# Hand-overs between normed stages: row sums kept with tokens on partitions, the factor spread by scaled identities, own rooms for two weight units

## The chip, the core and the metric

One core of a Trainium2 chip runs the whole program. The metric is device time in microseconds (us) of one execution. Before the change, three timed executions took 3216.22, 3218.62 and 3218.68 us; the median is 3218.62.

## The reference

Two transformer blocks of depth 2 run one after the other on one sequence of T = 512 tokens, model width D = 1024, in float32. The first (`ffn1`, `mix`, `ffn2`, twice) is not touched. The second has four stages, each of the form

```
h = h + rms_norm(f(rms_norm(h, gain_pre)), gain_post)
rms_norm(x, g) = x * rsqrt(mean(x * x over the 1024 channels) + 1e-6) * g
f: diff  differential attention (w_qkv, w_o)
   conv_0  h @ w_in (1024 x 5632), causal conv of width 3, gelu(gate) * val, @ w_out (2816 x 1024)
   fox   forgetting attention with shared keys, values and gates (w_kvf, w_q, w_o)
   conv_1  as conv_0
```

So between two stages two norms follow each other: the *post* norm of what the stage gave, added to the residual stream, and the *pre* norm of the sum, which feeds the next stage's products. The output is the stream after `conv_1`.

## The kernel before

Activations lie with channels on partitions: `xres`, `acc`, `h_hi` and `h_lo` are [128, 8, 512], eight channel blocks (k) of 512 tokens. Each product is made in three passes, high weight by high input, high by low, low by high, so ScalarE (`hi`, L817) copies a raw weight unit into its high part and VectorE (`lo`, L1293) subtracts to get the low part. A unit `c` is one 128-column block of a weight matrix; units are numbered through the program, and a unit's raw room, high and low rooms and PSUM bank are those of `c % 2`. SyncE issues the load of unit c when `lo` of unit c-2 is done (`load`, L539). `hi(c)` waits until TensorE is done with unit c-2, whose rooms it takes. Every engine works through one program order written out by hand; semaphores join them.

A pre norm is applied late: TensorE multiplies the un-normed `h_hi`/`h_lo` = gain times x, and the factor `rstd` (one per token, the same on all partitions) multiplies the result when VectorE takes it out of PSUM (`divided`, L1399). A post norm needs its factor `rstd2` at once.

The three hand-overs (`diff` to `conv_0`, `conv_0` to `fox`, `fox` to `conv_1`; `CHAINED` and `HALVED` name the stages before and after) and the end after `conv_1` run in two halves of 256 tokens:

- TensorE, `finish` (L1986): the last two output units, first for tokens 0 to 255, then for 256 to 511 (L2011). In the second part, at block nk//2, it issues `half_stat` for the first half, and behind its end `half_stat` for the second. `half_stat` (L1977, L1983) sums squares over channels: a full matrix of ones (weights) times [128 x 256] squares, so all 128 partitions hold the sum of each token. GpSimd has summed the squares of the first six blocks in `ssq`; ScalarE squares the last two (`half_square`, L869).
- ScalarE, `half_root` (L879): square root on [128 x 256]. VectorE, `half_invert` (L1358, L1362): reciprocal on [128 x 256].
- Then, block by block: VectorE makes `norm_t` = acc * gain * rstd2 (`post`, L1383), GpSimd adds it to `xres` (L800), ScalarE makes `h_hi` (L858) and the squares of the new x (L860), VectorE makes `h_lo` (`half_low`, L1334), three blocks behind `norm_t`.
- TensorE, `gemm_halves` (L1942): units c and c+1 of the next stage block by block as `h_lo` comes, with the pre norm's statistics between them, the second unit two blocks behind the first. Then unit c+2 in full width (`gemm`, L1905).

VectorE's order in `post` (L1365) holds `half_take` (the last two output units' halves out of PSUM, L1348 or L1350), the reciprocals and the low parts of units c and c+1; ScalarE's order in `finish` (L882) holds the matching squares, roots and high parts. After `conv_1`, TensorE transposes x (L2430), ScalarE copies it out of PSUM (L1268) and SyncE stores it.

## Time and profile before

| | |
|---|---|
| median of three timed executions | 3218.62 us |
| span of the profiled execution | 3216.7 us |
| TensorE busy (matmuls) | 3158.3 us, 98% of the span |
| VectorE / ScalarE / GpSimd busy | 54% / 36% / 17% |
| hand-over diff to conv_0 (2149.7 to 2190.7) | 41.0 us, granted clock 0.92 |
| hand-over conv_0 to fox (2527.1 to 2570.7) | 43.6 us, granted clock 0.96 |
| hand-over fox to conv_1 (2802.9 to 2843.8) | 40.9 us, granted clock 0.92 |
| end (3180.3 to 3216.7) | 36.4 us, granted clock 0.82 |

The profiled execution's own time outside the profiler is not given apart from the three; its span is 1.9 us under their median and 0.5 above the shortest. A hand-over is read here from the first half-width matmul of the old stage's last two units to the first full-width matmul of unit c+2 of the new stage. Times of a row are its start and its duration; matmuls overlap in the pipeline, so their spacing is read from start to start.

### The profile page before, as it was taken

What the parts mean: (1) busy time and instruction counts of PE and PEld (TensorE: products, weight loads), DVE (VectorE), ACT (ScalarE), POOL (GpSimd) and SP (SyncE); (2) the same over time, 40 slices, a digit from 0 to 9 for tenths busy, and PEclk for the clock granted to TensorE, in tenths of its full rate; (3) what the DMA queues carried; (4) which work ended last, traced back from release to release, by engine and by line L of the source; (5) the groups of instructions that cost most, each with busy time, mean ns of one, the idle gap of its engine ahead of it and who ended that gap; (6) DMA issues with size and microseconds to landing.
All of it is one profiled execution on the core that took longest, in us unless ns stands there. A gap on an engine that the chain in (4) does not pass through costs nothing.

```text
span 3216.7 us, 42242 instructions
## 1 busy us (share of the span) xinstructions
PE 3158.3 (98%) x14778; PEld 2537.6 (79%) x14778; DVE 1744.4 (54%) x2707; ACT 1160.1 (36%) x1880; POOL 534.5 (17%) x482
## 2 busy tenths in 40 slices
PE   8999999999999999999999999999999999999998
PEld 6888876788888888776888878668888886778887
DVE  4434477543445434585543453557656546586474
ACT  4323246322223222354322232644324335443242
POOL 0000336200020000265100030231000422310004
PEclk9999999999999999999999999999999999999999
DMA  4355331333333333321333323112333231223332
GB/s 122 97 143 148 95 108 36 89 97 93 98 98 93 104 91 106 80 60 47 94 104 90 108 76 118 47 55 77 107 88 102 66 103 40 60 72 104 92 96 81
DMA packets 528363, 288.01 MB, mean 90 GB/s; under 512 B 13603, under 2 KB 520198, under 8 KB 528256
## 3 DMA queue, kind: packets, MB, share of 16 engines
q1 hardware_dynamic: 523648, 273.32, 29.4%
q0 software_dynamic: 4608, 13.30, 1.4%
q8 instruction: 62, 1.02, 0.1%
q14 instruction: 45, 0.37, 0.0%
HBM read 284.30 MB, written 10.02 MB: 91 GB/s over the span
## 4 chain that ended last, share of the span: by engine, by line
PE 86%; DVE 7%; issue 3%; ACT 3%; POOL 1%; DMA 0%; DVEq 0%; ACTq 0%; POOLq 0%
PE bank L1905 66%; PE bank L1918 5%; PE bank L2075 3%; PE bank L2185 2%; PE bank L1935 2%; PE bank L2227 2%; PE bank L2250 1%; PE bank L2011 1%; PE bank L1964 1%; DVE w_lo L1293 1%; ACT w_hi L817 1%; PE bank L1983 1%; DVE scaled_g L1399 0%; DVE tap_g L1488 0%; DVE norm_t L1383 0%
## 5 line engine op out<-in xcount | busy, mean ns | idle before, releaser
L817 ACT ACTIVATE w_hi<-w_raw 128x1024 fp32r<-128x1024 f32 (+2 forms) x477 | 534.0, 1119 | 1419.3 <-PE bank L1905 718.8
L1905 PE MATMUL bank<-h_hi,w_hi 128*128 128x512 f32 x2420 | 949.2, 392 | 7.4 <-DVE h_lo L1323 3.7
L1905 PE MATMUL bank<-h_hi,w_lo 128*128 128x512 f32 x2420 | 942.4, 389 | 0.0
L1905 PE MATMUL bank<-h_lo,w_hi 128*128 128x512 f32 x2408 | 937.7, 389 | 0.0
L1293 DVE TENSOR_TENSOR w_lo<-w_raw,w_hi 128x1024 fp32r<-128x1024 f32 (+1 forms) x445 | 616.0, 1385 | 526.1 <-ACT w_hi L817 526.1
L1905 PEld LDWEIGHTS bank<-h_hi,w_hi 128*128 128x128 f32 x2420 | 453.7, 187 | 115.1 <-issue 14.7
L1905 PEld LDWEIGHTS bank<-h_hi,w_lo 128*128 128x128 f32 x2420 | 453.8, 188 | 95.9
L1905 PEld LDWEIGHTS bank<-h_lo,w_hi 128*128 128x128 f32 x2408 | 451.7, 188 | 95.5 <-issue 1.9
L1905 PE MATMUL bank<-act_hi,w_hi 128*128 128x512 f32 x924 | 360.3, 390 | 0.0
L1905 PE MATMUL bank<-act_lo,w_hi 128*128 128x512 f32 x924 | 360.0, 390 | 0.0
L1905 PE MATMUL bank<-act_hi,w_lo 128*128 128x512 f32 x924 | 359.9, 390 | 0.0
L1905 PEld LDWEIGHTS bank<-act_hi,w_hi 128*128 128x128 f32 x924 | 173.8, 188 | 36.3 <-issue 0.2
L1905 PEld LDWEIGHTS bank<-act_lo,w_hi 128*128 128x128 f32 x924 | 173.9, 188 | 36.2
L1905 PEld LDWEIGHTS bank<-act_hi,w_lo 128*128 128x128 f32 x924 | 173.8, 188 | 36.2
L1419 DVE SCALAR_TENSOR_TENSOR xres<-bank,xres 128x512 f32 (+1 forms) x64 | 44.2, 691 | 248.0 <-PE bank L1905 248.0
L1399 DVE TENSOR_TENSOR scaled_g<-bank,rstd 128x512 f32<-128x512 f32 x132 | 91.2, 691 | 149.6 <-PE bank L1905 144.8
L660 POOL TENSOR_TENSOR ssq<-xres 128x512 f32<-128x512 f32 x6 | 6.2, 1041 | 969.8 <-DVE xres L1419 945.8
L938 ACT ACTIVATE gated<-scaled_g 128x512 f32<-128x512 f32 x88 | 55.6, 632 | 297.3 <-DVE scaled_g L1399 297.2
L663 POOL TENSOR_TENSOR ssq<-ssq,psq 128x512 f32<-128x512 f32 x62 | 135.9, 2191 | 4.9
L1464 DVE TENSOR_TENSOR prod<-gate_r,bank 128x512 f32<-128x512 f32 x88 | 60.5, 687 | 99.2 <-PE bank L1905 99.0
L660 POOL TENSOR_TENSOR ssq<-acc 128x512 f32<-128x512 f32 x4 | 4.2, 1040 | 636.4 <-DVE acc L1426 619.2
L718 POOL TENSOR_TENSOR w_lo<-w_raw,w_hi 128x1024 fp32r<-128x1024 f32 x32 | 76.8, 2399 | 184.7 <-ACT w_hi L817 184.7
(333 smaller groups left out, 4160.8 us busy)
## 6 DMA issues: line engine op xcount, KB each, us to landing
w_raw<-in_ffn_w_gate_dram SPq DMA_DIRECT2D x88, 512.0 KB, 3.8
w_raw<-in_ffn_w_up_dram SPq DMA_DIRECT2D x88, 512.0 KB, 3.8
w_raw<-in_ffn_w_down_dram SPq DMA_DIRECT2D x64, 704.0 KB, 4.6
w_raw<-in_ffn_w_in_dram SPq DMA_DIRECT2D x88, 512.0 KB, 3.8
w_raw<-in_ffn_w_out_dram SPq DMA_DIRECT2D x32, 704.0 KB, 4.7
w_raw<-in_w_in_dram SPq DMA_DIRECT2D x34, 512.0 KB, 3.8
w_raw<-in_a_w_qkv_dram SPq DMA_DIRECT2D x24, 512.0 KB, 3.8
w_raw<-in_w_out_dram SPq DMA_DIRECT2D x16, 512.0 KB, 3.8
```

The source lines that it names most:

```text
L663: add = nc.gpsimd.tensor_tensor(ssq[:, :], ssq[:, :], psq[:, :], ALU.add)
L718: nc.gpsimd.tensor_tensor(w_lo[c % 2][:, 0:KT, :], raw[c % 2][:, 0:KT, :], w_hi[c % 2][:, 0:KT, :].bitcast(f32), ALU.subtract).then_inc(lo ...
L817: nc.scalar.activation(split_home(c)[0][:, 0:nk, 0:cols], raw[c % 2][:, 0:nk, 0:cols], ACT.Copy).then_inc(hi_ready, 1)
L1293: nc.vector.tensor_tensor(w_low[:, 0:nk, 0:cols], raw[c % 2][:, 0:nk, 0:cols], w_high[:, 0:nk, 0:cols].bitcast(f32), ALU.subtract).then_in ...
L1399: nc.vector.tensor_tensor(dst, result(c)[rows, :], rstd[rows, :], ALU.mult).then_inc(bank_free[c % 2], 1)
L1464: nc.vector.tensor_tensor(prod[:, :], gate_r[:, :], result(at + 1)[:, :], ALU.mult).then_inc(bank_free[(c + 1) % 2], 1)
L1905: mm = nc.tensor.matmul(result(c)[0:cols, :], w[:, k, 0:cols], x[k], start=(k == 0 and n == 0), stop=(k == nk - 1 and n == 2))
L1918: mm = nc.tensor.matmul(bank[c % 2][:, :], w[c % 2][:, k, :], x[k], start=(k == 0 and n == 0), stop=(k == KT - 1 and n == 2))
L1935: mm = nc.tensor.matmul(result(u)[:, :], w[u % 2][:, k, :], x[k], start=(k == 0 and n == 0), stop=(k == nk - 1 and n == 2))
L2075: mm = nc.tensor.matmul(V_BANK[t][:, :], x[:, k, tok], of_block[w][j], start=(k == 0 and n == 0), stop=(k == KT - 1 and n == 2))
L2185: mm = nc.tensor.matmul(PAIR_S[x][:, at:at + w], job["q"][:, P * i:P * (i + 1)], job["k"][:, first:first + w], start=True, stop=alone)
L2227: mm = nc.tensor.transpose(TURN[s % 2][:, to:to + P], ring_of(stage)[(2 * p + x) % 4][:, col:col + P], ident[:, :])
```

## The change

At the four places, not elsewhere:

- The statistic is turned. The squares are now the weights (128 channels x 128 tokens) and one column of `mean_p` (every value 1/128) is the moving operand, so the sum of each token lands on that token's partition, one PSUM column for 128 tokens. A block of a half takes two such matmuls instead of one with 256 columns.
- The root works on [128 x 2], the reciprocal too (`norm_tok`). VectorE then makes two scaled identities, diag(factor), in `rms`, and TensorE multiplies a matrix of ones with them (`half_spread`), which puts the factor on all partitions again, in PSUM. The post norm's `norm_t` reads the factor from PSUM there (`SPREAD_POST`); for the pre norm ScalarE copies it to `rstd` (`spread_copy`).
- Units c and c+1 of the next stage get rooms of their own (`home`), laid over the bias tables, so their `hi` waits for no matmul. `hi` and `lo` of both units move ahead of the first half's root and reciprocal; those of unit c+2 move into `finish` and to the end of `post`. On GpSimd `fox`'s writes into that area wait for the first two units.
- In the hand-overs the post norm's second statistic and its spread move from the end of `finish` into `gemm_halves`, to blocks 3 and 6 of the first half; the pre norm's spreads stand behind block 7 of the second half and at block 3 of unit c+2. `half_take` of the second half moves to blocks 1 and 4 of the first. The output transposes use banks 3, 4, 0, 1 instead of 3 to 6.

```diff
@@ -227,6 +232,9 @@
 bias_diff = put("bias_diff", [P, 8, T], bias_at + 4 * HA * NEAR)
+home = [[put(f"home_{part}{i}", [P, KT, P], bias_at + 4 * D * (2 * n + i), f32r) for i in range(2)]
+        for n, part in enumerate(("hi", "lo"))]
+HOMES = {BASE[n] + i for n in HALVED for i in range(2)}
@@ -340,8 +349,11 @@
 HALF = [slice(0, T // 2), slice(T // 2, T)]
-STAT_HALF = [STATB[:, HALF[0]], OUT[:, HALF[1]]]
+STAT_TOK = [STATB[:, T // 2:T // 2 + 2], OUT[:, 0:2]]
+SPREAD_POST = [bank[5][:, HALF[0]], bank[6][:, HALF[1]]]
+SPREAD_NEXT = [STATB[:, HALF[0]], OUT[:, HALF[1]]]
 EARLY_HALF = [bank[3], bank[4]]
+Y_BANK = [bank[3], bank[4], bank[0], bank[1]]
@@ -404,6 +417,8 @@
+if c in HOMES:
+    return home[0][c % 2], home[1][c % 2]
@@ -761,6 +776,7 @@
 pool.wait_ge(o_ready, OUTB["fox"])
+pool.wait_ge(mm_done, BASE["fox"] + 2)
@@ -811,8 +827,8 @@
     act.wait_ge(*also)
-if c >= 2 and c not in THIRD:
-    act.wait_ge(mm_done, c - 1 + 2 * j)
+if c >= 2 and c not in THIRD and c not in HOMES:
+    act.wait_ge(mm_done, c - (3 if c - 2 in HOMES else 1) + 2 * j)
@@ -869,38 +885,49 @@
-def half_root(event, n, half):
+def half_root(event, half):
...
         act.wait_ge(sum_ready, STAT[event] + 1)
-    nc.scalar.activation(rms[:, HALF[half]], STAT_HALF[half], ACT.Sqrt, bias=eps_c[:, 0:1],
-                         scale=1.0 / n).then_inc(rms_ready if half else rms_first, 1)
+    nc.scalar.activation(norm_tok[:, int(event in BASE), 2 * half:2 * half + 2], STAT_TOK[half], ACT.Sqrt,
+                         bias=eps_c[:, 0:1], scale=P / D).then_inc(rms_ready if half else rms_first, 1)
+def spread_copy(name, half):
+    act.wait_ge(spread_done, SPREAD_DONE[name, half])
+    nc.scalar.activation(rstd[:, HALF[half]], SPREAD_NEXT[half],
+                         ACT.Copy).then_inc(rstd_ready if half else rstd_first, 1)
 def finish(name):
...
     half_square(name, 0, 0)
+    hi(c)
+    hi(c + 1)
     half_square(name, 0, 1)
-    half_root("post_" + name, D, 0)
-    hi(c)
+    half_root("post_" + name, 0)
     half_square(name, 1, 0)
-    hi(c + 1)
-    half_square(name, 1, 1)
     following = NEXT.get(name)
     if following is None:
-        half_root("post_" + name, D, 1)
+        half_square(name, 1, 1)
+        half_root("post_" + name, 1)
         return
...
             if half == 0 and k == 2:
-                half_root("post_" + name, D, 1)
+                half_square(name, 1, 1)
+            if half == 0 and k == 4:
+                half_root("post_" + name, 1)
+            if half == 1 and k == 2:
+                half_root(following, 0)
             if half == 1 and k == 4:
-                half_root(following, D, 0)
+                hi(c + 2)
+    spread_copy(following, 0)
 def act_high(jj):
@@ -1170,13 +1197,15 @@
     token_root()
-hi(c + 2)
+if name not in HALVED:
+    hi(c + 2)
...
 elif name in HALVED:
+    half_root(name, 1)
     hi(c + 3)
-    half_root(name, D, 1)
+    spread_copy(name, 1)
@@ -1265,7 +1294,7 @@
 act.wait_ge(y_turned, 2 * t + a + 1)
-nc.scalar.activation(ytok[:, t, T * a:T * (a + 1)], bank[3 + 2 * (t % 2) + a][:, :],
+nc.scalar.activation(ytok[:, t, T * a:T * (a + 1)], Y_BANK[2 * (t % 2) + a][:, :],
@@ -1350,17 +1379,17 @@
-def half_invert(event, half):
-    dst = (rstd if event in BASE else rstd2)[:, HALF[half]]
+def half_diag(event, half):
+    tok = norm_tok[:, int(event in BASE), :]
...
         dve.wait_ge(rms_first, HALF_ROOT[event] + 1)
-        nc.vector.reciprocal(dst, rms[:, HALF[0]]).then_inc(rstd_first, 1)
-        dve.wait_ge(rstd_first, HALF_ROOT[event] + 1)
...
         dve.wait_ge(rms_ready, ROOT[event] + 1)
-        nc.vector.reciprocal(dst, rms[:, HALF[1]]).then_inc(rstd_ready, 1)
-        dve.wait_ge(rstd_ready, ROOT[event] + 1)
+    chain(nc.vector.reciprocal(tok[:, 2 * half:2 * half + 2], tok[:, 2 * half:2 * half + 2]))
+    for t in (2 * half, 2 * half + 1):
+        ins = nc.vector.tensor_scalar(rms[:, P * t:P * (t + 1)], ident[:, :], tok[:, t:t + 1], None, ALU.mult)
+    ins.then_inc(diag_ready if half else diag_first, 1)
 def post(name, how):
@@ -1368,30 +1397,37 @@
     half_take(name, how, 0, 0)
+    lo(c)
     half_take(name, how, 0, 1)
-    half_invert("post_" + name, 0)
-    half_take(name, how, 1, 0)
-    lo(c)
+    lo(c + 1)
+    half_diag("post_" + name, 0)
+    dve.wait_ge(rstd_first, HALF_ROOT["post_" + name] + 1)
     lag = 3
...
         for k in range(KT + lag):
+            if half and k == 0:
+                if name not in NEXT:
+                    half_diag("post_" + name, 1)
+                dve.wait_ge(rstd_ready, ROOT["post_" + name] + 1)
             if k < KT:
...
                     dve.wait_ge(x_done, X_FIRST[name] + k - 3)
-                nc.vector.scalar_tensor_tensor(norm_t[k % 4][:, tok], acc[:, k, tok], gain(g, l, k), rstd2[:, tok],
+                nc.vector.scalar_tensor_tensor(norm_t[k % 4][:, tok], acc[:, k, tok], gain(g, l, k), SPREAD_POST[half],
                                                ALU.mult, ALU.mult).then_inc(t_ready if half else t_first, 1)
-            if half == 0 and k == 2:
+            if half == 0 and k == 1:
+                half_take(name, how, 1, 0)
+            if half == 0 and k == 4:
                 half_take(name, how, 1, 1)
...
                 half_low(NEXT[name], k - lag, half)
-            if half == 0 and k == 4:
-                lo(c + 1)
-            if half == 0 and k == 6:
-                half_invert("post_" + name, 1)
+            if half == 0 and k == 8 and name in NEXT:
+                half_diag("post_" + name, 1)
+            if half == 1 and k == 7 and name in NEXT:
+                half_diag(NEXT[name], 0)
     if name in NEXT:
-        half_invert(NEXT[name], 0)
+        lo(c + 2)
 def divided(c, dst, j=0, rows=slice(0, P)):
@@ -1780,13 +1816,15 @@
     continue
-lo(c + 2)
+if name not in HALVED:
+    lo(c + 2)
...
 elif name in HALVED:
+    half_diag(name, 1)
     lo(c + 3)
-    half_invert(name, 1)
+    dve.wait_ge(rstd_ready, ROOT[name] + 1)
@@ -1891,7 +1929,7 @@
 def _(pe):
-    def gemm(c, x_hi, x_lo, ready, count, j=0):
+    def gemm(c, x_hi, x_lo, ready, count, j=0, midway=None):
@@ -1900,6 +1938,8 @@
 for k in range(nk):
+    if midway is not None and k == 3:
+        half_spread(midway, 1)
@@ -1945,6 +1985,12 @@
 for k in range(KT + lag):
+    if half == 0 and k == 3:
+        half_stat("post_" + before, 1, [b[:, HALF[1]] for b in sq_last])
+    if half == 0 and k == 6:
+        half_spread("post_" + before, 1)
+    if half == 1 and k == KT:
+        half_spread(name, 0)
     if k < KT:
@@ -1960,30 +2006,45 @@
 def half_block(c, k, tok, last):
     cols = UNIT[c][1]
-    for n, (w, x) in enumerate(((w_hi, h_hi), (w_hi, h_lo), (w_lo, h_hi))):
-        mm = nc.tensor.matmul(result(c)[0:cols, tok], w[c % 2][:, k, 0:cols], x[:, k, tok],
+    w_high, w_low = split_home(c)
+    for n, (w, x) in enumerate(((w_high, h_hi), (w_high, h_lo), (w_low, h_hi))):
+        mm = nc.tensor.matmul(result(c)[0:cols, tok], w[:, k, 0:cols], x[:, k, tok],
                               start=(k == 0 and n == 0), stop=(k == KT - 1 and n == 2))
...
 def half_stat(event, half, blocks, at=0, n=None):
-    if half == 0 and at == 0:
+    summed = event in POOL_SUM
+    if half == 0 and summed:
         stat_free(event)
-    summed = event in POOL_SUM
     if summed:
...
             pe.wait_ge(ssq_ready, POOL_SUM[event] + 1)
-        nc.tensor.matmul(STAT_HALF[half], ones[:, :], ssq[:, HALF[half]], start=True, stop=False)
+        for j in range(2):
+            nc.tensor.matmul(STAT_TOK[half][:, j:j + 1], ssq[:, P * (2 * half + j):P * (2 * half + j + 1)],
+                             mean_p[:, 0:1], start=(j == 0), stop=False)
     for k, b in enumerate(blocks, at):
...
             pe.wait_ge(sq_ready, SQ_FIRST[event] + k + 1)
-        mm = nc.tensor.matmul(STAT_HALF[half], ones[:, :], b, start=(k == 0 and not summed),
-                              stop=(k == (n or len(blocks)) - 1))
+        for j in range(2):
+            mm = nc.tensor.matmul(STAT_TOK[half][:, j:j + 1], b[:, P * j:P * (j + 1)], mean_p[:, 0:1],
+                                  start=(k == 0 and j == 0 and not summed),
+                                  stop=(j == 1 and k == (n or len(blocks)) - 1))
     if k == (n or len(blocks)) - 1:
...
+def half_spread(event, half):
+    pe.wait_ge(diag_ready if half else diag_first, (DIAG[event] if half else HALF_ROOT[event]) + 1)
+    mm = nc.tensor.matmul((SPREAD_NEXT if event in BASE else SPREAD_POST)[half], ones[:, :], rms[:, HALF[half]],
+                          start=True, stop=True)
+    if event in BASE:
+        mm.then_inc(spread_done, 1)
+    else:
+        mm.then_inc(rstd_ready if half else rstd_first, 1)
 def finish(name, x_hi, x_lo, ready, count):
@@ -2005,13 +2066,17 @@
                 pe.wait_ge(ready, count + k + 1)
-                if (half, s, k) == (1, 0, nk // 2):
+                if (half, s, k) == (1, 0, 3):
                     half_stat("post_" + name, 0, [b[:, HALF[0]] for b in sq_last])
+                if half and s * nk + k == 8:
+                    half_spread("post_" + name, 0)
...
             mm.then_inc(mm_done if half else half_done, 1)
-    half_stat("post_" + name, 1, [b[:, HALF[1]] for b in sq_last])
+    if name not in NEXT:
+        half_stat("post_" + name, 1, [b[:, HALF[1]] for b in sq_last])
+        half_spread("post_" + name, 1)
 def first_units(name, c, count):
@@ -2324,7 +2389,7 @@
 first_units(name, c, h0)
-gemm(c + 2, H_HI, H_LO, h_ready, h0)
+gemm(c + 2, H_HI, H_LO, h_ready, h0, midway=name if name in HALVED else None)
...
```

## Rows read from the trace of the kernel before

**Rows 1.** The page: the chain that ended last, share of the span by engine.

```profile
PE 86%; DVE 7%; issue 3%; ACT 3%; POOL 1%; DMA 0%; DVEq 0%; ACTq 0%; POOLq 0%
```

**Rows 2.** Windows: first and second hand-over; busy us (instructions) by engine, clock, DMA.

```profile
2149.70:2190.70 41.00, 36.52 (x238) 33.52 (x236) 32.00 (x44) 19.79 (x45) 17.50 (x18) 0.92 0.16 48
2527.10:2570.70 43.60, 40.12 (x273) 36.73 (x272) 32.32 (x44) 21.15 (x46) 22.62 (x24) 0.96 0.14 37
```

**Rows 3.** Windows: inside the first hand-over.

```profile
2164.00:2168.00 4.00, 1.79 (x9) 1.13 (x8) 3.65 (x7) 3.42 (x10) 3.64 (x5) 1.00 0.46 131
2168.00:2176.00 8.00, 6.15 (x24) 5.46 (x23) 7.96 (x13) 3.63 (x10) 2.84 (x5) 0.57 0.22 66
```

**Rows 4.** Waits of PE in the first hand-over: total, times, longest.

```profile
PE bank L1964 <- DVE h_lo L1334: 2.8, 3, 1.9
PE bank L1983 <- ACT sq_last L869: 1.3, 1, 1.3
PE bank L2011 <- DVE w_lo L1293: 0.3, 1, 0.3
```

**Rows 5.** Timeline of PE: start, duration, engine, line; a statistic, six products follow, then the next.

```profile
2184.63 0.59 PE L1983 MATMUL bank<-acc,ones 128*128 128x256 f32 x2
...
2185.65 0.28 PE L1964 MATMUL bank<-h_hi,w_lo 128*128 128x256 f32 x1
2185.77 0.38 PE L1983 MATMUL bank<-acc,ones 128*128 128x256 f32 x1
```

**Rows 6.** Timeline of PE in diff: eight one-column passes, and what follows.

```profile
2030.02 0.95 PE L2117 MATMUL bank<-mean_p,proj 128*128 128x1 f32 x8
2030.90 0.59 PE L2185 MATMUL bank<-proj 64*128 64x384 f32 x2
```

**Rows 7.** Timeline of DVE in the first hand-over.

```profile
2159.51 1.75 DVE L1358 RECIPROCAL rstd<-rms 128x256 f32<-128x256 f32 x1 [2.88 <-ACT rms L879]
...
2162.77 1.75 DVE L1383 SCALAR_TENSOR_TENSOR norm_t<-acc,gains,rstd 128x256 f32<-128x256 f32 x3
...
2167.44 1.75 DVE L1293 TENSOR_TENSOR w_lo<-w_raw,w_hi 128x1024 fp32r<-128x1024 f32 x1
```

**Rows 8.** Timeline at the program's start: DVE's small reciprocal, scaled identities; ACT's small root.

```profile
28.18 0.18 DVE L1755 RECIPROCAL tok_sum<-tok_sum 128x4 f32<-128x4 f32 x1 [4.58 <-ACT tok_sum L1143]
28.39 0.88 DVE L1757 TENSOR_SCALAR rms<-ident,tok_sum 128x128 f32<-128x128 f32 x4
...
27.86 0.28 ACT L1143 ACTIVATE tok_sum<-tok_sum,eps_c 128x4 f32<-128x4 f32 x1
```

**Rows 9.** Timeline of ACT and DVE in the first hand-over: the two parts of the input.

```profile
2165.91 0.49 ACT L858 ACTIVATE h_hi<-xres,gains 128x256 fp32r<-128x256 f32 x1
...
2167.05 0.47 DVE L1334 SCALAR_TENSOR_TENSOR h_lo<-xres,gains,h_hi 128x256 fp32r<-128x256 f32 x1
```

**Rows 10.** Timeline of SP: load of unit c+1's raw weights; the page: loads' time to landing.

```profile
2153.13 0.37 SPq L539 DMA_DIRECT2D w_raw<-in_ffn_w_in_dram  x1
...
w_raw<-in_ffn_w_in_dram SPq DMA_DIRECT2D x88, 512.0 KB, 3.8
```

**Rows 11.** Timeline of DVE and POOL: norm_t, then a PSUM-reading add, each beside POOL.

```profile
2181.38 0.96 DVE L1383 SCALAR_TENSOR_TENSOR norm_t<-acc,gains,rstd 128x256 f32<-128x256 f32 x1
2181.14 0.91 POOL L800 TENSOR_TENSOR xres<-xres,norm_t 128x256 f32<-128x256 f32 x1 [0.36 <-DVE norm_t L1383]
...
2544.46 0.42 DVE L1350 TENSOR_TENSOR acc<-bank,acc 128x256 f32<-128x256 f32 x1 [0.21 <-PE bank L2011]
2543.05 2.46 POOL L800 TENSOR_TENSOR xres<-xres,norm_t 128x256 f32<-128x256 f32 x3 [11.08 <-DVE norm_t L1383]
2545.88 0.73 POOL L800 TENSOR_TENSOR xres<-xres,norm_t 128x256 f32<-128x256 f32 x1 [0.36 <-DVE norm_t L1383]
```

**Rows 12.** Timeline of DVE and POOL at the end.

```profile
3202.23 6.94 DVE L1383 SCALAR_TENSOR_TENSOR norm_t<-acc,gains,rstd 128x256 f32<-128x256 f32 x9
...
3202.79 7.64 POOL L800 TENSOR_TENSOR xres<-xres,norm_t 128x256 f32<-128x256 f32 x9 [0.99 <-DVE norm_t L1383]
```

More of the change, by code:

```diff
@@ L137, in program @@
     HALF_ROOT, HALF_SQ, half_squares = {}, {}, 0
+    DIAG = {}
     STAT, ROOT, POOL_SUM, SQ_FIRST, X_FIRST, NEXT = {}, {}, {}, {}, {}, {}
@@ L149, in program @@
             HALF_ROOT[n], HALF_SQ[n] = len(HALF_ROOT), half_squares
+            DIAG[n] = HALF_ROOT[n]
             half_squares += KT
@@ L167, in program @@
             HALF_ROOT["post_" + n], HALF_SQ["post_" + n] = len(HALF_ROOT), half_squares
+            DIAG["post_" + n] = HALF_ROOT["post_" + n]
             half_squares += 2
             X_FIRST[n] = KT * len(X_FIRST)
+    SPREAD_DONE = {(n, half): 2 * i + half + 1 for i, n in enumerate(HALVED) for half in range(2)}
     T_FIRST = {n: KT * i for i, n in enumerate(n for n in stages if n in CHAINED)}
@@ L297, in program @@
         own_rows = put("own_rows", [P, 2, NP])
+        norm_tok = put("norm_tok", [P, 2, NT])
         ident, ones = put("ident", [P, P]), put("ones", [P, P])
@@ L366, in program @@
         sum_ready, rms_ready, rstd_ready = sem("sum_ready"), sem("rms_ready"), sem("rstd_ready")
+        diag_first, diag_ready, spread_done = sem("diag_first"), sem("diag_ready"), sem("spread_done")
         t_ready, hhi_ready, h_ready = sem("t_ready"), sem("hhi_ready"), sem("h_ready")
@@ L2404, in _ @@
                     first_units(name, c, h0)
-                    gemm(c + 2, H_HI, H_LO, h_ready, h0)
+                    gemm(c + 2, H_HI, H_LO, h_ready, h0, midway=name)
                     gemm(c + 3, H_HI, H_LO, h_ready, h0)
@@ L2429, in _ @@
                             wait_x(pe, stages[-1], k)
-                        mm = nc.tensor.transpose(bank[3 + 2 * (t % 2) + a][:, P * (k % 4):P * (k % 4 + 1)],
+                        mm = nc.tensor.transpose(Y_BANK[2 * (t % 2) + a][:, P * (k % 4):P * (k % 4 + 1)],
                                                  xres[:, k, P * t:P * (t + 1)], ident[:, :])
```

## The prediction

> **What bounds the kernel now.** Read first the chain that ended last: 86% of the span is TensorE [rows 1], so a microsecond of TensorE work, added or removed, counts in full, and what can be won are TensorE's gaps. The windows give the first two hand-overs 41.0 and 43.6 us [rows 2]; the third, 40.9 at a clock of 0.92, is like the first and stands in the table of times. To see how much of that is gap I work out TensorE's full-speed work there. From one statistic's start to the next, with six half-width products between, is 1.14 us; the last product starts 0.12 before the next statistic, so six products take 0.72 and a statistic (two passes) 0.42 to 0.43 [rows 5]. The first hand-over has 2 x 2 x 8 x 3 = 96 half-width products in the old stage's last two units, 96 in the new stage's first two, and 3 + 3 + 16 = 22 statistics: 192 x 0.12 + 22 x 0.43 = 32.5. The second has 11 blocks in the old units, so 228 x 0.12 + 9.5 = 36.8. The third equals the first. Gap: 8.5, 6.8 and 8.4, together 23.7 us.
>
> Where it lies shows in two views. The waits name 4.4 us in the first hand-over: 2.8 for `h_lo`, 1.3 for the square of the last block, 0.3 for a low weight part [rows 4]. The other 4 us stand in no wait. After 2164 TensorE was busy 1.8 of 4 us, and in the next 8 us its granted clock was 0.57 [rows 3], that is mostly the lower of its two levels, 1.2 of 2.4 GHz: products cost double there. Over whole hand-overs the granted clock was 0.92, 0.96 and 0.92 [rows 2], 3.3 + 1.7 + 3.3 = 8.3 us, part of the 23.7. VectorE was busy 7.96 of those 8 us [rows 3]: it was the late one.
>
> **The change, step by step** (first hand-over; the profiled span, 3216.7, is 1.9 below the median, and I take the difference found there off the median).
>
> *Root and reciprocal small.* A reciprocal on 128x256 took 1.75 [rows 7], on 128x4 0.18; a scaled identity 0.88/4 = 0.22; the small root 0.28 [rows 8]. Root, reciprocal and two identities come to 0.28 + 0.18 + 0.44 = 0.9, plus hand-overs between engines, against 1.75 for the reciprocal and a root at half width before it. Then TensorE spreads in two passes like a statistic, 0.43.
>
> *TensorE's added work.* Statistics: eight one-column passes take 2030.02 to 2030.90 = 0.88 [rows 6]; a block of a half needs four, 0.44 against 0.43. So the turned statistic saves TensorE nothing; 66 of them cost up to 1.0 more in all. Spreads: 4 per hand-over, 12 x 0.43 = 5.2. Sum 6.2 us on the path.
>
> *Earlier factor.* `hi` of unit c+1 now stands ahead of the second half-square in ScalarE's queue. Its load is issued at 2153.13 and lands 3.8 later, 2156.9 [rows 10]; a high part and the square, some 1.5 together, end at 2158.4. TensorE reaches that square at 2153.0 + 24 x 0.12 + 9 x 0.12 + 0.88 = 2157.9: a new stall of 0.5. In the second hand-over the old units are 36 products longer, the load is in, and nothing waits. The statistic ends at 2158.85, root and identities at 2160.0, the spread is issued at block 8, 2160.65, and the first `norm_t` can start at 2161.3 instead of 2162.8 [rows 7]. The low parts of c and c+1 (1.75 for the one that stood in the middle of the chain at 2167.44 [rows 7]) now end before the factor is there: VectorE waited then, so they cost nothing.
>
> *The feed of `gemm_halves`.* The old units end at 2164.0 (one spread later than before). `norm_t` 2161.3 plus 0.47, GpSimd 0.73 [rows 11], `h_hi` 0.49 and `h_lo` 0.47 [rows 9], with what ScalarE has queued, gives 2164.2: 0.2 stall. But VectorE's `half_take` of the last unit stands at block 4, ahead of the second `h_lo`, and cannot start before that unit's products are out, 2164.6. Then 0.42 + 0.47 for `h_lo` 1 and 0.94 for `norm_t` 5 and `h_lo` 2: TensorE waits 1.0 and 0.6. From block 2 on it has 1.15 of work per block against 0.95 to 1.28 for VectorE. In the second half `hi(c+2)`, about 1.1 in ScalarE's row, holds back block 5; with the diagonal's 0.6 in VectorE's I count 0.6 (0.3 to 1.2). The second spread waits for TensorE's own block 6; from there to the second half's first `h_lo` takes 2.9, TensorE still has 2 x 1.15 + 2 x 0.8 = 3.9: covered, by 1.0.
>
> Left over: 0.3 + 0.5 + 0.2 + 1.6 + 0.6 = 3.2 in the first and third, 0.95 + 0.6 + 0.6 = 2.15 in the second, where the factor is early. Together 8.5. With idle never over 1.0 at a time and TensorE busy over half of every 2 us, I take it that the clock stays up.
>
> *After it.* `lo(c+2)` ends before c+2 is due. Spread and copy of the pre norm's second half lie in unit c+2, 0.43 of which I counted; the factor is out some 3.2 us after that unit's start, before it was 3.9. GpSimd's new wait in `fox` holds back only writes of tables that are read long after.
>
> *`norm_t` from PSUM.* With both tensors in SBUF it took 0.96 beside GpSimd's add, which itself took 0.91; a VectorE add with one operand in PSUM took 0.42 beside a busy GpSimd, and GpSimd's shorter adds are 0.73 [rows 11]. So the bounds for `norm_t` are 0.42 and 0.96; I take 0.47. The Trainium skill (SBUF — State Buffer, "Who interferes with whom") says that a VectorE instruction with two SBUF inputs contends with a GpSimd one that reads SBUF and one with at most one doesn't. The rows agree. By its rule in full the pace in the second halves would be GpSimd's alone; that is the case "no gap left" below.
>
> *End.* The same steps for `conv_1`: the factor of the first half comes about 1.2 sooner, which the wait for the last unit swallows. The second half can start when the last unit is out (0.43 later than before), squared and summed: 3199.5, root and diagonals 3200.9, spread 3201.35, `norm_t` 3201.5. Before, nine `norm_t` in 6.94 from 3202.23 [rows 12] put the second half's first at 3203.0. From there GpSimd paces: nine in 7.64 is 0.85 each [rows 12]. Gain 1.5 plus 0.2 of 0 to 1.0 for a faster GpSimd: 1.7. The two spreads are inside this.
>
> **Sum.** 23.7 - 8.5 - 6.2 + 1.7 = 10.7 us less: 3218.6 - 10.7 = 3208.
>
> **Rivals.**
> 1. *No gap left.* `half_take` is not late because `norm_t` runs at 0.42 and GpSimd at 0.73, and ScalarE's extra high part hides. Left over only 0.3 twice: 23.7 - 0.6 - 6.2 + 2.7 = 19.6, 3199. For: the low add of rows 11. Against: the wait for the last unit's products is no matter of pace.
> 2. *The clock still falls.* The waits shrink to my 8.5 but the clock drops for the same stretches, 8.3 more: 3216, no change that can be measured. For: it fell after 2.2 us of idle in 4 [rows 3], and my stalls are 1.8 within 2.6 us. Against: TensorE works again at full rate right behind them. The Trainium skill (TensorE: Matmul & The Clock Gate, "What's actually happening") says that the throttled state is the default and that activity releases it; by that rule the full clock is not safe while waits remain, which is this rival's time, and no row tells at which of the two my shorter waits end.
> 3. *Slower: the feed is no faster, the work is.* Place: the loop ScalarE, VectorE, TensorE, VectorE that each factor now runs, with TensorE in order. If it and the late `half_take` give back what the small reciprocals save, the gaps stay at 23.7 and 6.2 come on top, with 0.9 at the end: 3226. It is slower from the point where gaps shrink by less than 6.2 of 23.7. Against: VectorE alone loses 5 us of reciprocals and 1.75 of a low part per hand-over from the busy stretch.
>
> **Chances.** Forecast 0.60 (its own range 3203 to 3212, nearly all faster), rival 1 0.14, rival 2 0.17, rival 3 0.09. A change under 0.2%, 6.4 us, can't be told from none: faster means below 3212.2. Faster 0.57 + 0.14 = 0.71 and 0.01 of rival 2: 0.72; same 0.03 + 0.16 = 0.19; slower 0.09. Range 3199 to 3216: it leaves out rival 3, half of rival 1 and a little of rival 2.
>
> **What would show it.** Right: hand-overs of about 38, 41.6 and 38 us; granted clock near 1.0 in them; root and reciprocal rows of 0.2 to 0.3; `norm_t` near 0.47 beside GpSimd; waits for `h_lo` under 2 us per hand-over, right behind the `half_take` at block 4; statistics of 0.44. Wrong: a clock of 0.5 after the first `h_lo`; long waits of `norm_t` in the second half for the spread; a wait over 1 us at the first statistic because a load lands late; statistics well above 0.44.

## The result, and the profile after

| | before | after |
|---|---|---|
| median of eight executions each | 3217.62 us | 3226.39 us |
| range | 3216.22 to 3218.68 | 3223.74 to 3228.63 |
| ratio after/before | | 1.0028, 95% interval 1.0019 to 1.0037 |
| span of the profiled execution | 3216.7 | 3223.5 |

The kernel became slower by 8.8 us, clear of the noise by its interval, where 3208 was forecast with a range of 3199 to 3216.

The windows of the three hand-overs after the change, in the columns of [rows 2]: from the first half-width product of the old stage's last two units to the first full-width product of unit c+2.

```profile
2147.30:2189.30 42.00, 39.91 (x288) 38.76 (x287) 24.69 (x50) 18.59 (x47) 15.97 (x18) 0.88 0.21 59
2526.00:2578.10 52.10, 51.35 (x324) 50.49 (x323) 23.87 (x51) 20.27 (x48) 16.38 (x18) 0.74 0.16 41
2810.60:2852.70 42.10, 39.98 (x288) 38.81 (x287) 24.77 (x50) 20.00 (x48) 16.12 (x18) 0.88 0.20 59
```

Before they took 41.0, 43.6 and 40.9 us [rows 2, and the table of times]; now 42.0, 52.1 and 42.1. Read the first number behind the length (TensorE busy) against the number behind the five busy times (granted clock): TensorE idles for 2.1, 0.75 and 2.1 us where [rows 2] show 4.5 and 3.5 in the first two, and VectorE's work fell from 32 to under 25 us. The gaps that the change was to close are half of what they were or less. But the clock is 0.88, 0.74 and 0.88 instead of 0.92, 0.96 and 0.92. At 0.5 for the lower level (1.2 of 2.4 GHz) that is 42.0 x 0.12 + 52.1 x 0.26 + 42.1 x 0.12 = 23.6 us lost, against 8.3 before.

The waits of TensorE in the first hand-over, to be held against [rows 4]:

```profile
PE bank L2011 <- DVE h_lo L1363: 1.3, 3, 0.9
PE bank L2033 <- ACT sq_last L885: 0.4, 1, 0.4
PE bank L2074 <- DVE w_lo L1322: 0.3, 1, 0.3
```

2.0 us instead of 4.4. Inside the first hand-over (the same place as [rows 3]), and then the second, cut at the places where the clock changes:

```profile
2162.00:2164.00 2.00, 0.94 (x6) 0.77 (x6) 2.00 (x6) 2.00 (x7) 1.31 (x2) 1.00 0.00 0
2164.00:2168.00 4.00, 3.84 (x30) 3.63 (x28) 2.18 (x6) 1.38 (x5) 2.64 (x3) 0.85 0.00 0
2168.00:2176.00 8.00, 8.00 (x38) 7.82 (x37) 3.08 (x10) 1.62 (x5) 0.72 (x2) 0.50 0.00 0
...
2526.00:2549.00 23.00, 22.25 (x184) 21.77 (x183) 13.22 (x25) 11.03 (x24) 9.97 (x10) 1.00 0.26 69
2549.00:2576.00 27.00, 27.00 (x126) 26.73 (x125) 10.64 (x26) 8.54 (x23) 6.41 (x8) 0.50 0.08 20
2576.00:2578.10 2.10, 2.10 (x17) 1.99 (x16) 0.02 (x1) 0.70 (x3) 0.00 (x0) 0.90 0.00 0
```

In the kernel before, the clock stood at half for some 6.6 us of the first hand-over (41.0 x 0.08 x 2) and came back. Now the second hand-over spends 27 us at half clock with TensorE busy in every one of them. VectorE, busy 7.96 of 8 us in [rows 3], is busy 3.1 of 8 here: at half clock TensorE itself is the late one. The sign that the prediction gave for being wrong, a clock of 0.5 after the first `h_lo`, is there.

A statistic and its six products, at full clock and at half, from TensorE's timeline (start, duration); from one statistic's start to the next it is 1.16 us at full clock, against 1.14 in [rows 5], and 2.13 at half clock:

```profile
2180.66 0.50 PE L2033 MATMUL bank<-mean_p,acc 128*128 128x1 f32 x4
...
2181.82 0.50 PE L2033 MATMUL bank<-mean_p,acc 128*128 128x1 f32 x4
...
2170.00 0.85 PE L2033 MATMUL bank<-mean_p,acc 128*128 128x1 f32 x4
...
2172.13 0.85 PE L2033 MATMUL bank<-mean_p,acc 128*128 128x1 f32 x4
```

VectorE in the first hand-over (to be held against [rows 7, 8, 11]): small reciprocal, two scaled identities, `norm_t` from PSUM, `half_take` at block 4 with the `h_lo` behind it, and the second half's first `norm_t`.

```profile
2157.06 0.17 DVE L1389 RECIPROCAL norm_tok<-norm_tok 128x2 f32<-128x2 f32 x1
2157.26 0.48 DVE L1391 TENSOR_SCALAR rms<-ident,norm_tok 128x128 f32<-128x128 f32 x2
2159.05 0.87 DVE L1417 SCALAR_TENSOR_TENSOR norm_t<-acc,gains,bank 128x256 f32<-128x256 f32 x2 [1.30 <-PE bank L2042]
...
2162.35 0.41 DVE L1377 TENSOR_SCALAR acc<-bank 128x256 f32<-128x256 f32 x1
2162.69 0.91 DVE L1363 SCALAR_TENSOR_TENSOR h_lo<-xres,gains,h_hi 128x256 fp32r<-128x256 f32 x1
...
2174.72 1.65 DVE L1417 SCALAR_TENSOR_TENSOR norm_t<-acc,gains,bank 128x256 f32<-128x256 f32 x4 [4.88 <-PE bank L2042]
```

The last row shows what the low clock does to the order: the spread stands in TensorE's own queue, so `norm_t` waits 4.88 us for it.

The end, from the first half-width product to the last instruction, took 3223.5 - 3189.45 = 34.05 us instead of 36.4: 2.35 less. e1 below, with 34.1 us there, has the same gain, so it does not hang on the clock in the hand-overs. Between the hand-overs each stage took 0.2 to 0.3 us more, probably part of the spread that lies in unit c+2. Up to the first hand-over this profiled execution was 2.4 us shorter than that of before, at a clock of 1.00 against 0.98 in its first 200 us; that is not of the change: e2 below, which is the kernel before up to that point, reached it 2.0 us sooner too (2147.7 against 2149.7). Together: +10.7 (hand-overs) + 0.9 - 2.35 - 2.4 = +6.8, the difference of the spans.

### The profile page after: what moved, and what is told of

It is laid out like the page before. It is cut to its first block, busy times and chain, and to the rows that moved or that the text cites. A ratio compares the mean times of both kernels' runs of the same rounds, so it can differ in the third digit from the quotient of the medians.

```text
span 3223.5 us, 42603 instructions
## 1 busy us (share of the span) xinstructions
PE 3174.0 (98%) x14950; PEld 2561.5 (79%) x14950; DVE 1712.4 (53%) x2735; ACT 1156.6 (36%) x1886; POOL 529.6 (16%) x482
## 4 chain that ended last, share of the span: by engine, by line
PE 87%; DVE 6%; issue 3%; ACT 3%; POOL 1%; DMA 0%; DVEq 0%; ACTq 0%; POOLq 0%; SPq 0%
PE bank L1945 66%; PE bank L1958 5%; PE bank L2140 3%; PE bank L2250 2%; PE bank L1975 2%; PE bank L2292 2%; PE bank L2011 2%; PE bank L2315 1%; PE bank L2074 1%; PE bank L2033 1%; ACT w_hi L833 1%; DVE w_lo L1322 1%; ACT tap_v L987 0%; DVE prod L1555 0%; DVE scaled_g L1435 0%
## 5 line engine op out<-in xcount | busy, mean ns | idle before, releaser
L833 ACT ACTIVATE w_hi<-w_raw 128x1024 fp32r<-128x1024 f32 (+1 forms) x471 | 527.6, 1120 | 1396.8 <-PE bank L1945 716.8
L1322 DVE TENSOR_TENSOR w_lo<-w_raw,w_hi 128x1024 fp32r<-128x1024 f32 (+1 forms) x439 | 607.2, 1384 | 517.8 <-ACT w_hi L833 517.7
```

The lines of the kernel that those rows point to most:

```text
L833: nc.scalar.activation(split_home(c)[0][:, 0:nk, 0:cols], raw[c % 2][:, 0:nk, 0:cols], ACT.Copy).then_inc(hi_ready, 1)
L1322: nc.vector.tensor_tensor(w_low[:, 0:nk, 0:cols], raw[c % 2][:, 0:nk, 0:cols], w_high[:, 0:nk, 0:cols].bitcast(f32), ALU.subtract).then_in ...
```

## Experiments

The waits shrank and the clock didn't stay up. Two things could hold it down: the new form of the statistics (one moving column per 128 x 128 weights, where 256 columns moved before), or the stalls at the first blocks, whatever the statistic's form.

**e1, wide operand.** All 128 equal columns of `mean_p` move, not one, into 128 PSUM columns; the root reads one column of each block.

```diff
-STAT_TOK = [STATB[:, T // 2:T // 2 + 2], OUT[:, 0:2]]
+STAT_WIDE = [STATB[:, HALF[1]], OUT[:, HALF[0]]]
+STAT_TOK = [STATB[:, T // 2:T:P], OUT[:, 0:T // 2:P]]
...
-mm = nc.tensor.matmul(STAT_TOK[half][:, j:j + 1], b[:, P * j:P * (j + 1)], mean_p[:, 0:1],
+mm = nc.tensor.matmul(STAT_WIDE[half][:, P * j:P * (j + 1)], b[:, P * j:P * (j + 1)], mean_p[:, :],
```

> The kernel after with one edit: the moving operand of each turned statistic is all 128 equal columns of mean_p instead of one, into 128 PSUM columns per token block instead of 1; the root reads one column of each block as before. In theory A (the one-column passes hold the granted clock at its lower level after the stalls of a hand-over) the stretches at half clock of the three hand-overs, some 10, 27 and 10 us in the kernel after, shrink to 5 us or less each, the windows of the three hand-overs fall from 42.0, 52.1 and 42.1 us to 38 to 40 each, and the time to 3200 to 3212 us (from 3226.4). In theory B (the stalls alone set how long it lasts, whatever the statistic's form) the stretches and the time stay: 3223 to 3229 us. A statistic should still take about 0.44 us per half block at full clock; were it longer by 0.2 the sum would be 13 us worse.

Measured: 3203.9 us, ratio 0.9960 (0.9946 to 0.9974). Its three hand-overs, the stretch with the stalls and the 12 us behind it in the first, the waits of TensorE there, and a statistic with six products:

```profile
2147.00:2184.20 37.20, 35.28 (x288) 34.13 (x287) 24.81 (x50) 18.51 (x47) 16.15 (x18) 1.00 0.23 67
2520.80:2560.30 39.50, 38.76 (x323) 38.14 (x322) 24.39 (x50) 20.15 (x47) 16.58 (x18) 1.00 0.20 54
2792.90:2830.10 37.20, 35.31 (x288) 34.17 (x287) 24.79 (x50) 19.95 (x48) 16.13 (x18) 1.00 0.23 67
...
2161.60:2163.60 2.00, 0.90 (x5) 0.73 (x6) 2.00 (x6) 2.00 (x7) 1.35 (x2) 1.00 0.00 0
2163.60:2167.60 4.00, 3.83 (x34) 3.63 (x32) 2.20 (x7) 1.38 (x5) 2.65 (x3) 1.00 0.00 0
2167.60:2175.60 8.00, 8.00 (x70) 7.95 (x69) 6.44 (x17) 4.94 (x15) 4.26 (x6) 1.00 0.01 2
...
PE bank L2012 <- DVE h_lo L1364: 1.4, 3, 0.9
PE bank L2075 <- DVE w_lo L1323: 0.3, 1, 0.3
PE bank L2034 <- ACT sq_last L886: 0.3, 1, 0.3
...
2170.93 0.61 PE L2034 MATMUL bank<-mean_p,acc 128*128 128x128 f32 x4
...
2172.09 0.61 PE L2034 MATMUL bank<-mean_p,acc 128*128 128x128 f32 x4
```

The same instructions but for the width, the same waits to 0.1 us, the same 1.16 us from statistic to statistic, and the clock is 1.00 in all three. The hand-overs are 4.8, 12.6 and 4.9 us shorter than after the change, 22.3 of the 22.5 us between the medians. The one-column operand cost no time of its own, and with it the clock fell. Stalls of this size (TensorE busy 0.90 of 2 us here, 0.94 after the change) don't make it fall by themselves. Larger ones may: see e9.

**e2, the kernel before with one-column passes.** In its statistics all but the first pass of a sum are two one-column matmuls instead of one with 256. The sums that come of it are wrong, so this kernel computes other factors, and its values differ from there on; it is for timing only.

```diff
-mm = nc.tensor.matmul(STAT_HALF[half], ones[:, :], b, ...)
+for j in range(2):
+    mm = nc.tensor.matmul(STAT_HALF[half][:, j:j + 1], b[:, P * j:P * (j + 1)], ones[:, 0:1], start=False, ...)
```

> The kernel before with one edit: in the statistics of the hand-overs all passes of 256 columns but the first of each sum are replaced by two one-column passes, so that the factors are not the reference's; order, roots, reciprocals and waits stay. Theory A: the low-clock stretches of the hand-overs (6.6, 4 and 6 us before) become 10 us or longer, and the time rises by 5 to 20 us to 3222 to 3238. Theory B: at full clock both forms take 0.43 to 0.44 us, so the time stays at 3217 to 3219 us and the clock of the hand-overs at 0.92, 0.96 and 0.92.

Measured: 3223.99 us (3222.05 to 3236.51), ratio 1.0026 (1.0017 to 1.0035).

```profile
2147.70:2195.00 47.30, 42.81 (x273) 41.38 (x271) 31.72 (x44) 19.48 (x45) 17.44 (x18) 0.78 0.14 41
2531.40:2575.10 43.70, 40.39 (x310) 39.10 (x309) 32.33 (x44) 21.13 (x46) 22.62 (x24) 0.92 0.14 37
2807.30:2848.20 40.90, 36.39 (x274) 35.04 (x272) 31.98 (x44) 21.18 (x46) 17.49 (x18) 0.92 0.17 48
```

The first hand-over, 41.0 before, takes 47.3 with some 20 us at half clock; the second spends some 7 us there (43.7 x 0.08 x 2), twice as long as before, and the third the same as before. It goes the way of the first theory in the other kernel too, but not in every hand-over: what the one-column passes do there depends on something that these rows don't show. Nor does it separate the operand's width from the other values.

**e3, statistics and factors as before, the rest as after.** Ones times 256 columns, root and reciprocal on 128x256, no spreads; rooms and order stay.

```diff
-half_diag("post_" + name, 0)
+half_invert("post_" + name, 0)
...
-half_spread("post_" + name, 0)
...
-nc.vector.scalar_tensor_tensor(norm_t[k % 4][:, tok], acc[:, k, tok], gain(g, l, k), SPREAD_POST[half],
+nc.vector.scalar_tensor_tensor(norm_t[k % 4][:, tok], acc[:, k, tok], gain(g, l, k), rstd2[:, tok],
```

> The kernel after with statistics, roots, reciprocals and factors as before (a matrix of ones times 256 columns of squares, root and reciprocal on 128x256, no spreads, factor in SBUF); rooms of their own, the earlier high and low parts, and the order of squares, statistics and half_take stay as in the kernel after. It prices the turned part against the order. Theory A: no one-column pass is left, so the half-clock stretches are 7 us or less; the post factor comes later by the reciprocal (1.75 us against 0.9 with the spread), TensorE does 5.2 us less: 3208 to 3220 us. Theory B: the clock stays low as long as in the kernel after, 23.6 us lost in the three hand-overs, and only the 5.2 us go: 3219 to 3226 us.

Measured: 3213.88 us, ratio 0.9990 (0.9981 to 0.9999). The first and third hand-over take 41.9 and 40.7 us, at 0.92 and 0.96, the second 40.6 at 1.00; TensorE waits 3.9 us for `h_lo` in the first, where e1 waits 1.4. VectorE's rows show why:

```profile
2157.40 1.75 DVE L1390 RECIPROCAL rstd<-rms 128x256 f32<-128x256 f32 x1 [0.41 <-ACT rms L897]
...
2177.92 0.96 DVE L1431 SCALAR_TENSOR_TENSOR norm_t<-acc,gains,rstd 128x256 f32<-128x256 f32 x1
```

So the turned statistic with a wide operand, its small root and reciprocal and its factor in PSUM are together worth 3213.88 - 3203.9 = 10 us, in spite of the spreads. Part of the 10 is clock: 41.9 x 0.08 + 40.7 x 0.04 = 5.0 us, where e1 loses none. No one-column statistic is left in e3, and its clock falls for some us all the same, behind a longer stall than e1's (1.4 us against 0.9).

**e4, a mix.** Post norms turned with the wide operand, pre norms (whose factor is not urgent) as before: half of the spreads and all the copies go.

```diff
 def half_root(event, half):
+    if event in BASE:
+        nc.scalar.activation(rms[:, HALF[half]], STAT_HALF[half], ACT.Sqrt, bias=eps_c[:, 0:1], scale=1.0 / D)...
+        return
...
-    half_diag(NEXT[name], 0)
+    half_invert(NEXT[name], 0)
```

> The kernel after with the post norms' statistics turned at 128 columns (as in the run with the wide operand) and the pre norms' statistics and factors as before (ones times 256 columns, root and reciprocal on 128x256, no spread and no copy): 6 spreads of 0.43 us less than the wide version, no one-column pass left. Theory A: as the wide version less 2 to 3 us: 3198 to 3209 us. Theory B: the kernel after less 2.6 us: 3221 to 3226 us.

Measured: 3203.36 us, ratio 0.9958 (0.9944 to 0.9971). Its hand-overs are 36.6, 38.75 and 36.5 us, 2.0 less than in e1 together, the clock 1.00; the medians differ by 0.5, which their intervals don't tell apart.

**e5 and e6, which statistics?** e5 moves 128 columns in the post norms' statistics alone, e6 in the pre norms' alone. The cut is shown against e1; the first pass of a post norm's sum, over `ssq`, has 128 columns in e5 and one in e6.

```diff
+w = 1 if event in BASE else 128     # e6: 128 if event in BASE else 1
-mm = nc.tensor.matmul(STAT_WIDE[half][:, P * j:P * (j + 1)], b[:, P * j:P * (j + 1)], mean_p[:, :],
+mm = nc.tensor.matmul(STAT_WIDE[half][:, P * j:P * j + w], b[:, P * j:P * (j + 1)], mean_p[:, 0:w],
```

> The kernel after with 128 moving columns only in the post norms' statistics (12 per hand-over pass group: ssq and the last two squares of each half), one column in the 16 of the pre norm. Theory A1 (the clock falls because the cluster of post statistics at block 3 follows the stalls at blocks 0 to 2; what comes later only delays the recovery): no fall, hand-overs 37 to 40 us, 3202 to 3208 us. Theory A2 (the one-column statistics of the pre norm, one per block through the whole of gemm_halves, do it): the stretches at half clock stay 5 us or longer, 3212 to 3228 us.

> The mirror of the run before: one column in the post norms' statistics, 128 in the pre norm's. Theory A1: the clock falls at block 3 as in the kernel after, but recovers after 4 to 7 us as in the kernel before, since only wide statistics follow: clock of the hand-overs 0.92 to 0.96, 3208 to 3216 us. Theory A2: no fall or a short one: 3203 to 3208 us.

Measured: e5 3204.39 us (0.9962, 0.9949 to 0.9975), e6 3202.85 us (0.9958, 0.9945 to 0.9971). e6's clock is 1.00 in all three hand-overs, e5's in the first two; its third is

```profile
2792.80:2831.50 38.70, 36.83 (x287) 35.70 (x286) 24.76 (x50) 19.96 (x48) 16.12 (x18) 0.96 0.22 64
```

1.5 us longer than e1's. The first theory (the post statistics start the fall) fits e5 and not e6, the second (those of the pre norm do it) fits e6 and not e5. So neither holds as put: widening either group almost suffices. Only with both kinds in one column is the clock lost as in the kernel after.

**e7, stalls filled.** One-column statistics kept, ten extra half-width products ahead of the first three waits.

```diff
 if half == 0:
+    for _ in range((2, 7, 1)[k] if k < 3 else 0):
+        nc.tensor.matmul(bank[6][:, HALF[0]], home[0][c % 2][:, 0, :], home[1][c % 2][:, 0:2, :], start=True, stop=True)
     pe.wait_ge(h_first, T_FIRST[before] + k + 1)
```

> The kernel after, one-column statistics kept, with 10 half-width products (0.12 us each, into a PSUM half that nothing reads) put ahead of the first three waits for h_lo of each hand-over, 2, 7 and 1 of them, to fill the stalls of 0.31, 0.88 and 0.16 us. If the stalls are needed as the trigger, the clock stays near 1.0 with one-column statistics too: hand-overs 38 to 40 us, 3204 to 3210 us. If the one-column statistics alone pull it down, the clock falls all the same: 3222 to 3230 us.

Measured: 3212.52 us (3207.69 to 3227.7 in 12 executions), ratio 0.9996 (0.9985 to 1.0008): between the two answers. In the profiled execution the clock is 0.88, 0.85 and 1.00 in the three hand-overs. The second, cut where the clock changes:

```profile
2527.20:2549.00 21.80, 21.80 (x184) 21.73 (x183) 13.00 (x24) 10.13 (x20) 9.97 (x10) 1.00 0.28 73
2549.00:2552.00 3.00, 3.00 (x21) 3.00 (x21) 1.86 (x6) 2.37 (x7) 0.00 (x0) 0.74 0.02 5
2552.00:2564.00 12.00, 12.00 (x56) 11.79 (x56) 5.46 (x13) 4.21 (x12) 5.71 (x8) 0.50 0.00 1
2564.00:2573.00 9.00, 9.00 (x78) 8.95 (x78) 3.52 (x9) 3.54 (x10) 0.68 (x1) 1.00 0.22 60
```

TensorE is busy 45.8 of 45.8 us and waits for nothing, and still the clock falls, behind the post statistics of block 3. Idle time is not needed for the fall. The fill does make it shorter or rarer: the third hand-over kept its clock, single executions came down to 3207.7, and the median lies 13.9 us under that of the kernel after. Whether that is for the idle time gone or for the ten added products, which are 256 columns wide, this run does not tell.

**e8, the mix with `half_take` of the last unit behind the second `h_lo`.**

```diff
+                        if k >= lag and name in NEXT:
+                            half_low(NEXT[name], k - lag, half)
                         if half == 0 and k == 4:
                             half_take(name, how, 1, 1)
-                        if k >= lag and name in NEXT:
-                            half_low(NEXT[name], k - lag, half)
```

> The mix (post norms turned at 128 columns, pre norms with ones) with one more edit: half_take of the last unit's second half stands behind the second h_lo in VectorE's order at block 4, not ahead of it. By the prediction's step the wait of 0.88 us at the second block comes from that half_take, so it falls to 0.3 or less in the first and third hand-over and 0.6 to 0.2 in the second: 1.5 us less in all, 3201 to 3203 us. If VectorE is late there anyway, or ScalarE's h_hi of the fourth block is now held up by the square behind it, the wait only moves on: 3203 to 3205 us.

Measured: 3201.47 us, ratio 0.9950 (0.9938 to 0.9963), the lowest median of all. TensorE's timeline at the first three blocks (in brackets the idle time):

```profile
2162.99 0.35 PE L2022 MATMUL bank<-h_hi,home_hi 128*128 128x256 f32 x1 [0.31 <-DVE h_lo L1366]
2163.77 0.39 PE L2022 MATMUL bank<-h_hi,home_hi 128*128 128x256 f32 x1 [0.19 <-DVE h_lo L1366]
2164.89 0.39 PE L2022 MATMUL bank<-h_hi,home_hi 128*128 128x256 f32 x1 [0.50 <-DVE h_lo L1366]
```

Against e4 the wait at the second block falls from 0.87 to 0.19, as the step said, and half of that comes back at the third block (0.17 to 0.50). The hand-overs are 0.45, 0.4 and 0.3 us shorter than in e4. The medians differ by 1.9, but the intervals of e4 and e8 overlap; the gain rests on the waits and the hand-overs.

**e9, e1 without the rooms of their own.** High and low parts stand where they stood before, in the ordinary rooms, and `half_take` of the second half's first unit stands ahead of the loop again.

```diff
-HOMES = {BASE[n] + i for n in HALVED for i in range(2)}
+HOMES = set()
...
+half_take(name, how, 1, 0)
+lo(c)
 dve.wait_ge(rstd_first, HALF_ROOT["post_" + name] + 1)
...
+if half == 0 and k == 4:
+    lo(c + 1)
```

> The version with the wide operand (3203.9 us), with the rooms of their own taken back: the first two units of the next stage use the ordinary rooms again, so their high and low parts stand where they stood in the kernel before (high parts behind the first root, low part of c ahead of the loop, of c+1 at block 4, those of c+2 in the next stage), and half_take of the second half's first unit stands ahead of the loop. If the rooms and the order are worth what the prediction gave them (a low part of 1.75 us out of VectorE's row in front of norm_t, another at block 4), h_lo waits rise from 1.4 to 4 us or more in a hand-over and the time to 3211 to 3218 us, and with such stalls the clock may fall for some us. If the small reciprocals alone freed VectorE, it stays within 3203 to 3208 us.

Measured: 3223.1 us, ratio 1.0020 (1.0011 to 1.0029), worse than either answer.

```profile
2148.70:2191.50 42.80, 37.39 (x287) 36.06 (x285) 24.71 (x51) 19.89 (x47) 15.93 (x18) 0.92 0.16 45
...
PE bank L2006 <- DVE h_lo L1361: 4.1, 3, 2.7
```

The waits for `h_lo` go from 1.4 to 4.1 us, the longest from 0.9 to 2.7, and with them the clock falls though all statistics are wide (0.92, 0.96 and 0.92 in the three hand-overs). So there are two ways to lose it: long stalls with wide operands, and one-column statistics with short stalls or none. The rooms, and the order that they allow, carry 19 us of the wide version's gain. The three hand-overs are 18.0 us longer than in e1, and 8.7 of that is clock (42.8 x 0.08 + 45.8 x 0.04 + 43.3 x 0.08). Without the rooms the small reciprocals don't pay for their spreads.

## Why the prediction was wrong

The step that failed: "With idle never over 1.0 at a time and TensorE busy over half of every 2 us, I take it that the clock stays up." Both conditions were about met: the longest wait for `h_lo` was 0.9 us, and TensorE was busy 0.94 of 2 us in the thinnest stretch shown, 3.84 of the next 4. The clock fell all the same, for longer than before. What the runs showed in its place: with both kinds of statistics in one column the hand-overs lost 23.6 us to the clock; with all of them 128 columns wide and the same stalls they lost none (e1). The prediction had priced the statistics by time only, one-column passes 0.44 us and 256-column passes 0.43, hence "the turned statistic saves TensorE nothing". What the granted clock does behind them was not asked.

With the clock up (e1) the sum can be held against the runs: 10.7 us less were forecast, 3216.78 - 3203.9 = 12.9 measured against the kernel before on the same chip. Most of the 2 us between them come from the second hand-over (about 1) and the end (0.65).

- *Root, reciprocal, identities.* 0.9 forecast; 0.26 + 0.17 + 0.48 = 0.91 in the kernel after.
- *TensorE's added work.* Right: statistic to statistic 1.16 against 1.14; 66 x 0.02 = 1.3 for the forecast's "up to 1.0". In e1 a spread's two passes push the next-but-one product from 0.24 to 0.67 us behind the one before them: 0.43.
- *Earlier factor.* The first `norm_t` starts 2159.05 - 2147.30 = 11.75 us into the hand-over; 2161.3 - 2149.7 = 11.6 was forecast. The new stall at the first statistic: 0.4 (0.3 in e1) for 0.5.
- *The feed.* 0.3 at the first block for 0.2, 0.88 at the second for 1.0, 0.17 at the third for 0.6. The 0.6 counted for the second half did not come: e1 has no wait there. So the waits of e1's first hand-over are 2.0 us for a forecast of 3.2. Its work is 192 x 0.12 + 22 x 0.44 + 3 x 0.43 = 34.0, which leaves a gap of 37.2 - 34.0 = 3.2, the forecast's number; but 1.2 us of it stand in no wait and were in none of the forecast's terms, so that agreement is luck. In the second the gap is 39.5 - 38.3 = 1.2 for 2.15, with waits of 0.7 in all. The sign given for this hand-over, about 41.6 us, does not follow from the prediction's own terms: 36.8, 0.3 for the statistics, 4 x 0.43 and 2.15 make 41.0.
- *`norm_t` from PSUM.* 0.47 beside GpSimd, for 0.47; with both inputs in SBUF 0.96 (e3). The Trainium skill (SBUF — State Buffer, "Who interferes with whom") says that a VectorE instruction with two SBUF inputs contends with a GpSimd one that reads SBUF, and that one with at most one SBUF input, outside its two-port modes, does not. These two rows agree.
- *The second spread "covered, by 1.0".* True for TensorE in e1, which has no wait there, though `norm_t` waits 1.3 us for the spread; at half clock `norm_t` waited 4.88 us.
- *End.* 2.35 for 1.7 (2.3 in e1).

Rival 2, with a chance of 0.17, named the clock, but took the size from the stretches of before, 8.3 us; it was 23.6 in the kernel after, and e1's hand-overs put it at 22.3. Its cause was wrong too: it tied the fall to the waits, where e1 kept the clock with the same waits and e7's second hand-over lost it without any. Rival 3 came out at the measured time, 3226, for a reason that didn't happen, since the gaps shrank: its number is right by luck. The Trainium skill (TensorE: Matmul & The Clock Gate, "What's actually happening") says that the throttled state is the default and activity releases it. What the default is, no run here shows. But being busy by the profile's count did not bring the full clock back: TensorE was busy for 27 of 27 us at half clock in the kernel after.

What stays open: why the half-clock stretch ended after 10 us in the first and third hand-over and after 27 in the second, with the same statistics in all three. The second's first unit has 112 columns of weights in place of 128; that was not tried alone. Open is also why moving columns matter to the clock at all: e1 shows that they do in this kernel, and no run shows by what. It is no matter of one unlucky execution: the mean clock of the eight lay between 0.988 and 0.990, and that of e1's five between 0.996 and 0.997.

## What to carry to other kernels

Where a profile shows TensorE 100% busy at a granted clock of 0.5, the work takes about twice its time (2.13 us for 1.16 here): look at the clock column before the busy column, and where it is low, at the stalls before it and at how wide the moving operands are. When a matmul is turned so that its moving operand shrinks to one column, try it with more columns first; here 128 took no more time than one. And price a feed, its buffers and its operand shapes together: the rooms without the wide operand lost 8.8 us, the wide operand without the rooms lost 6, both together won 13, and with the cheaper pre norm and a later `half_take` 15.6 (the last step's medians not told apart by their intervals).

## What the hardware showed that was not expected

- 128x128 weights with 1 or with 128 moving columns in float32: the same spacing, 0.36 to 0.37 us from the statistic's start to the next product's, for four such matmuls as the trace merges them. In these rows the added columns cost nothing.
- The clock fell to half in a stretch in which TensorE had been busy for more than 20 us without a gap (e7), and stayed there for 27 us of unbroken work in the kernel after.
- In two of the versions with one-column statistics, executions of one program lie far apart: 3207.7 to 3227.7 in e7 and, for one execution of ten, 3236.5 against 3222.1 to 3225.7 in e2. In the kernel after they lie within 4.9 us, in e1 within 2.5.
